# Routed experts of a hybrid layer: another order of the experts, rows of 32 turned on VectorE, modulation ahead of the gather, results scaled in two steps

## The reference

```python
def hier_moe(h, ...):                       # h = modulate(x1, sh2, sc2): normalize(x1) * (1 + sc2) + sh2
    p_g, grp = lax.top_k(softmax(t @ w_rg + b_rg), 1)          # 4 groups of experts
    p_e, local = lax.top_k(softmax(logits_in), 2)              # two of the group's 8 experts
    gate = p_g * p_e / sum(p_e)
    ...
def block_ffn(xb, e):                       # rows of one expert, width 1024 -> 512 -> 1024
    return (silu(xb @ w_gate[e]) * (xb @ w_up[e])) @ w_down[e]
# y[token] = sum over its two experts of gate * block_ffn(row);  out = LayerNorm(ALPHA * x1 + g2 * y)
```

## Time and profile before

| | us |
|---|---|
| median of 3 runs | 1691.51 (1689.35 to 1691.93) |
| the profiled execution's own time | 1683.64 |
| its span, first to last instruction | 1681.9 |

### The profile page before, as it was taken

The page is one execution under the profiler, slowest core; times in us unless marked ns, Lnnn a source line. Parts: engine busy times, 40 slices in busy tenths (PEclk is TensorE's granted clock), DMA queues, the critical chain, the costliest instruction groups (busy, mean ns, idle before and its releaser), DMA issues. The chain is left out here.

```text
span 1681.9 us, 46845 instructions
## 1 busy us (share of the span) xinstructions
PE 1495.7 (89%) x19436; PEld 1102.2 (66%) x19436; DVE 927.6 (55%) x1855; ACT 694.2 (41%) x1585; POOL 209.9 (12%) x274
## 2 busy tenths in 40 slices
PE   5799998999977899986999989964999999998768
PEld 3578886779967788874666668852656565665433
DVE  6798762332115556558989957865151553444416
ACT  5444431012235455534767745532141433533311
POOL 0000001000034445324000000000000000000024
PEclk8899999999987999997999989985999999999989
DMA  9312324542133345213011024417849789999976
GB/s 369 114 63 95 100 79 161 201 157 76 50 108 116 109 116 142 85 54 122 20 44 51 7 92 176 163 67 287 350 166 379 268 333 418 414 420 418 370 259 242
DMA packets 115265, 305.31 MB, mean 182 GB/s; under 512 B 11010, under 2 KB 57682, under 8 KB 106074
## 3 DMA queue, kind: packets, MB, share of 16 engines
q1 hardware_dynamic: 93178, 244.95, 38.7%
q0 software_dynamic: 10336, 46.67, 7.8%
q10 hardware_dynamic: 11520, 10.49, 2.0%
HBM read 256.41 MB, written 45.67 MB: 180 GB/s over the span
## 5 line engine op out<-in xcount | busy, mean ns | idle before, releaser
L2753 PE MATMUL psum<-now_hidden,i_xm 128*32 128x256 f32 x4992 | 291.9, 387 | 13.0 <-DVE now_hidden L2863 12.2
L2753 PEld LDWEIGHTS psum<-now_hidden,i_xm 128*32 128x32 f32 x4992 | 162.1, 112 | 125.5 <-DVE now_hidden L2863 16.1
L2765 PE MATMUL psum<-now_down,i_hT 128*32 128x256 f32 x2464 | 147.1, 379 | 3.1 <-ACT now_down L2820 3.0
L2879 DVE TENSOR_TENSOR i_h<-i_silu,psum 128x128 f32<-128x128 f32 x78 | 22.2, 285 | 203.0 <-ACT i_silu L2813 203.0
L2863 DVE COPY now_hidden<-raw_hidden 128x1024 f32 x168 | 104.2, 691 | 27.1 <-DMA raw_hidden<-in_w_up 18.9
L2765 PEld LDWEIGHTS psum<-now_down,i_hT 128*32 128x32 f32 x2464 | 79.7, 110 | 57.2 <-ACT now_down L2820 5.0
L2803 ACT ACTIVATE i_xm<-psum,run_mod 128x128 f32<-128x128 f32 x163 | 63.2, 455 | 121.8 <-issue 81.8
L124 PE MATMUL psum<-hT_head,wm_head 128*128 128x512 f32 (+1 forms) x256 | 96.9, 378 | 11.2 <-DVE hT_rest L415 6.9
L1918 PE MATMUL psum<-dkT,f_qT 64*128 64x512 f32 (+1 forms) x384 | 89.7, 575 | 17.4 <-ACT f_E L1968 14.9
L1968 ACT ACTIVATE f_E<-psum,f_mx 128x1280 f32<-128x1280 f32 (+2 forms) x96 | 92.9, 972 | 18.6 <-DVE f_mx L2029 17.7
L124 PE MATMUL psum<-hT_head,wm_rest 128*128 128x512 f32 (+1 forms) x256 | 95.4, 373 | 0.0
(11 more groups left out here) (378 smaller groups left out, 3027.6 us busy)
## 6 DMA issues: line engine op xcount, KB each, us to landing
raw_hidden<-in_w_gate SPq DMA_DIRECT2D x22, 2048.0 KB, 24.9
raw_hidden<-in_w_up SPq DMA_DIRECT2D x22, 2048.0 KB, 30.4
raw_down<-in_w_down SPq DMA_DIRECT2D x22, 2048.0 KB, 21.1
wa_late<-in_w_ada POOLq DMA_DIRECT2D x16, 1024.0 KB, 5.6
yb<-i_y ACTq DMA_DIRECT2D x80, 128.0 KB, 10.0
wa<-in_w_ada SPq DMA_DIRECT2D x8, 1024.0 KB, 13.6
wt<-in_w_in SPq DMA_DIRECT2D x4, 2048.0 KB, 9.1
wm<-in_w_in SPq DMA_DIRECT2D x12, 512.0 KB, 4.0
```

Of the source, the lines that this page charges most:

```text
L2753: last = nc.tensor.matmul(by_blocks(hidden_bank(s)[j * SUB:(j + 1) * SUB, :]), xm[u][:, k, s * SUB:(s + 1) * SUB], columns_of(now["hidden" ...
L2765: last = nc.tensor.matmul(down_bank(s)[j * SUB:(j + 1) * SUB, :], hT[s % 2][:, k * SUB:(k + 1) * SUB], now["down"][:, k, j * WIDE:(j + 1) ...
```

## The change

1. **Order of the experts.** The place of rank `nth` among `used` experts is now found by dealing: row `nth // 6`, column `nth % 6`, read column by column (`STRIDE = 6`). For these inputs the blocks per place were 13, 1, 1, 11, 1, 1, 9, 1, 1, 7, 1, 5, 1, 5, 1, 4, 1, 4, 1, 3, 2, 4 and become 13, 4, 1, 1, 11, 4, 1, 1, 9, 4, 1, 1, 7, 3, 1, 1, 5, 2, 1, 5, 1, 1.
2. **Modulation.** GpSimd multiplies and adds the modulation in `mixed_output`, two operations of 128x1024 per tile, and SP stores their result to `xn2`. ScalarE's `shape` is gone.
3. **Rows.** A gather takes one block: 128 partitions, each with a quarter (256 numbers) of one of 32 tokens. VectorE turns it with one transpose of 128x256 in squares of 32x32 (`turn_x`), four blocks ahead; TensorE's transposes are gone. There are four buffers (`RING`) instead of two. `tok` is computed per block: 64 products with 32 rows of weights and 96 columns instead of 16 with 128 and 24.
4. **Results.** ScalarE copies a block's result from PSUM, GpSimd multiplies it by `rep_g` in place, and ScalarE waits for that before the next silu where it waited for VectorE before (in each fourth block, from block 64 on in each).
5. **Zeros.** `mixed_output` writes zeros to all eight quads of `yb` that may stay unused; nothing is written after the experts.

```diff
+LOW = 2 * SEQ // P
 COUNT = 96
+QUARTER = 70
+AHEAD = 4
+RING = SUBS
...
-                sp.wait_ge(x_normed, t + 1)
-                sp.dma_start(xn2[t], xn[t % 2][:, :]).then_inc(xn_stored[t % 2], 16)
+                sp.wait_ge(x_shaped, t + 1)
+                sp.dma_start(xn2[t], xs[t % 2][:, :]).then_inc(xn_stored[t % 2], 16)
...
+            for w in range(2):
+                sp.dma_start(late_mod[:, w, :], d["mod_rows"][3 + w:4 + w, :].to_broadcast([P, D])).then_inc(mod_loaded, 16)
...
+                if t == 1:
+                    sp.wait_ge(nothing_ready, 1)
+                if 1 <= t <= (QUADS - LOW) // 2:
+                    for q in range(LOW + 2 * (t - 1), LOW + 2 * t):
+                        sp.dma_start(ybq[q], nothing[:, :]).then_inc(nothing_stored, 16)
...
+        def _(pool):
+            nc.gpsimd.memset(nothing[:, :], 0.0).then_inc(nothing_ready, 1)
+            pool.wait_ge(mod_loaded, 32)
+            nc.gpsimd.tensor_scalar(late_mod[:, 1, :], late_mod[:, 1, :], 1.0, None, ALU.add).then_inc(mod_ready, 1)
+            pool.wait_ge(mod_ready, 1)
+            for t in range(TL):
+                u = t % 2
+                pool.wait_ge(x_normed, t + 1)
+                if t >= 2:
+                    pool.wait_ge(xn_stored[u], 16 * (t // 2))
+                nc.gpsimd.tensor_tensor(xs[u][:, :], xn[u][:, :], late_mod[:, 1, :], ALU.mult).then_inc(x_scaled, 1)
+                pool.wait_ge(x_scaled, t + 1)
+                nc.gpsimd.tensor_tensor(xs[u][:, :], xs[u][:, :], late_mod[:, 0, :], ALU.add).then_inc(x_shaped, 1)
...
-        link(ts(some_long[:, :], nblk[:, :], LONG - 0.5, None, ALU.is_gt))
-        link(red(threes[:, :], some_long[:, :], AX, ALU.add))
-        link(ts(by_three[:, :], used[:, :], 1.5, -0.5, ALU.mult, ALU.add))
-        link(stt(by_two[:, :], used[:, :], 2.0, threes[:, :], ALU.mult, ALU.subtract))
-        link(ts(by_two[:, :], by_two[:, :], -1.0, None, ALU.add))
+        nearest(whole[:, :], used[:, :], 1.0 / STRIDE, 0.5 / STRIDE - 0.5)
+        link(stt(left[:, :], whole[:, :], -float(STRIDE), used[:, :], ALU.mult, ALU.add))
+        tt(used_number[:, :], number, some[:, :], ALU.mult)
...
-        ts(short[:, :], nth, -1.5, by_three[:, :], ALU.mult, ALU.add)
-        ts(key[:, :], nth, -2.0, by_two[:, :], ALU.mult, ALU.add)
-        link(ts(pos[:, :], nth, 2.0, threes[:, :], ALU.mult, ALU.add))
-        link(tt(short[:, :], short[:, :], key[:, :], ALU.max))
-        link(stt(pos[:, :], nth, 3.0, pos[:, :], ALU.mult, ALU.min))
-        link(tt(pos[:, :], pos[:, :], short[:, :], ALU.min))
-        link(ts(pos[:, :], pos[:, :], -0.25, None, ALU.add))
-        link(ts(pos[:, :], pos[:, :], EXACT, None, ALU.add))
-        link(ts(pos[:, :], pos[:, :], -EXACT, None, ALU.add))
+        nearest(row_of[:, :], nth, 1.0 / STRIDE, 0.5 / STRIDE - 0.5)
+        link(stt(column_of[:, :], row_of[:, :], -float(STRIDE), nth, ALU.mult, ALU.add))
+        link(stt(pos[:, :], column_of[:, :], left[:, :], row_of[:, :], ALU.min, ALU.add))
+        link(stt(pos[:, :], column_of[:, :], whole[:, :], pos[:, :], ALU.mult, ALU.add))
...
+            tt(row_hot[:, here, :], is_row[:, here, :], ids[:, :].unsqueeze(2).to_broadcast([P, TL, SUB]), ALU.mult)
+            tt(part_hot[:, here, :], part_of[:, here].unsqueeze(2).to_broadcast([P, TL, BLOCKS]),
+               small[:, COUNT:COUNT + BLOCKS].unsqueeze(1).to_broadcast([P, TL, BLOCKS]), ALU.is_equal).then_inc(picked, 1)
...
-        cp(tok[:, 0:QUADS], m.bank(2, QUADS)).then_inc(token_ready, 1)
+        ts(tok[:, 0:BLOCKS], m.bank(2, BLOCKS), float(SUBS), small[:, QUARTER:QUARTER + 1], ALU.mult, ALU.add).then_inc(token_ready, 1)
...
-            last = nc.tensor.matmul(m.bank(2, QUADS), row_hot[:, n, :], part_hot[:, n, :], start=(n == 0), stop=(n == PICKS - 1))
+            for a in range(SUBS):
+                last = nc.tensor.matmul(m.bank(2, BLOCKS)[a * SUB:(a + 1) * SUB, :], row_hot[:, n, :], part_hot[:, n, :], start=(n == 0), stop=(n == PICKS - 1),
+                                        tile_position=(0, a * SUB))
...
-        def gather(q, i, u):
-            pool.wait_ge(x_turned[u], i)
-            pool.indirect_dma_start(out=xg[u][:, :], out_offset=None, in_=d["xn2"],
-                                    in_offset=bass.IndirectOffsetOnAxis(ap=tok[:, q:q + 1], axis=0)).then_inc(gathered[u], 16)
+        def gather(b):
+            pool.wait_ge(x_turned, b - RING + 1)
+            pool.indirect_dma_start(out=xg[b % RING][:, :], out_offset=None, in_=quarters(d["xn2"]),
+                                    in_offset=bass.IndirectOffsetOnAxis(ap=tok[:, b:b + 1], axis=0)).then_inc(gathered[b % RING], 16)
+
+        def scale(b, u, s):
+
+            pool.wait_ge(y_kept, b + 1)
+            nc.gpsimd.tensor_tensor(yo[u][:, s, :], yo[u][:, s, :], rep_g[:, :], ALU.mult).then_inc(y_scaled, 1)
+
+        def body(q, i, u, s):
+            b = q * SUBS + s
+            gather(b + AHEAD + RING)
+            scale(b, u, s)
 
         pool.wait_ge(routed, 1)
-        nc.gpsimd.memset(nothing[:, :], 0.0).then_inc(nothing_ready, 1)
-        blocks(pool, start=lambda q, i, u: gather(q + 2, i + 1, u))
+        pool.wait_ge(gate_loaded, 16 * SUBS)
+        for b in range(AHEAD):
+            gather(b + RING)
+        nb = blocks(pool, block=body)
+        for u in range(RING):
+            pool.wait_ge(gathered[u], ((nb + AHEAD + 2 * RING - 1 - u) >> 2) * 16)
...
+        def keep_y(b, i, u, s):
+            act.wait_ge(used["down"], b * KE + KE)
+            if s == 0:
+                act.wait_ge(stored[u], 16 * SUBS * i)
+            nc.scalar.activation(yo[u][:, s, :], down_bank(s), ACT.Copy).then_inc(y_kept, 1)
...
-        def keep_y(b, i, u, s):
-            dve.wait_ge(used["down"], b * KE + KE)
-            if s == 0:
-                dve.wait_ge(stored[u], 16 * SUBS * i)
-            nc.vector.tensor_tensor(yo[u][:, s, :], down_bank(s), rep_g[:, :], ALU.mult).then_inc(y_kept, 1)
...
+        def turn_x(b):
+
+            dve.wait_ge(gathered[b % RING], 16 * (b // RING) + 16)
+            if b >= RING:
+                dve.wait_ge(used["hidden"], (b - RING + 1) * KD)
+            nc.vector.transpose(xm[b % RING][:, :, :], run_columns(xg[b % RING])).then_inc(x_turned, 1)
...
-            keep_y(b, i, u, s)
+            turn_x(b + AHEAD)
```

133 lines of the change are left out of this document (50 added, 83 removed).

## The result

The changed kernel takes 1712.46 us (median of 4 runs, 1711.14 to 1719.63) against 1690.43 us of the kernel before in the same session: ratio 1.0152, 95% interval 1.0124 to 1.018. A second session, with the same kernel unedited, gave 1.0098 (1.0075 to 1.0121; medians 1707.85 against 1689.02). These ratios are not the quotients of the two medians, which would be 1.0130 and 1.0111. So the changed kernel is slower by 1.0 to 1.5%; the medians lie 22.0 and 18.8 us apart. 1679 was forecast. The two intervals do not overlap, so a ratio from one session and one from another can differ by half a per cent with no edit at all.

A forecast was written before the change was run, and what follows sets the result against it. TensorE (19.6 us per expert) and the weight queue (17.4) were taken as close bounds in the experts. Terms -14.8 + 1.0 + 1.7 + 0.3 - 0.6 + 0 = -12.4 us took 1691.51 to 1679.1; 8-in-10 range 1668 to 1692.

The forecast's parts named there:

- 3.7 us: Inside an expert block, the chain from silu through transposes and gather issue to GpSimd's multiplication; 1.5 us spare, costed at nothing.
- The exclusion: GpSimd's block operations and VectorE's weight copies getting in each other's way in SBUF: +1.0 us, bounds 0 to 35.
- `mixed_output`, +2.0: In `mixed_output`, +1.7 us for 1 MB loaded earlier at the start, +0.3 for a later store at the end.
- The experts, -14.8: From the experts to `combine`: earlier end without TensorE's transposes and with the new order, less the longer result path, -14.8 us.
- the 28.4 available: Between expert blocks, twenty sets of TensorE transposes at 1.42 us, all that removing them can give: 28.4 us.
- the replay: Block-by-block model of the experts' weight queue; put TensorE's end near 1601.5 us, 16 earlier, 3 of them from the order.
- Combine would begin at 1613.3.: Behind the experts, `combine` beginning 9.75 us after the first last store, at 1613.3 instead of 1628.12 us.
- the near 0 and -0.6: Routing: fewer small VectorE operations, -0.6 us; `tok` products and start of the first block, 0 (-3 to +6).
- The rival named last: In expert blocks, GpSimd's operations lengthened or held by VectorE's make ScalarE's silu late: +19.5 us, 1698.6; chance 0.12.

The follow-up runs named there:

- scaling on VectorE: Changed kernel with one VectorE operation taking the result from PSUM and multiplying it, replacing ScalarE's copy and GpSimd's multiplication; ratio 1.001 to the kernel before.
- one column: Changed kernel with GpSimd's multiplication of the result cut from 256 columns to one; ratio 1.0087 to the kernel before.
- the multiplication that nobody waits for: Changed kernel with the result scaled by VectorE, plus an unused GpSimd multiplication of 128x256 per block; ratio 1.0029 to the kernel before.

## Why the prediction was wrong

**"3.7 us, where ScalarE's next silu is due 5.18 us behind the last ... I cost it at nothing."** This step failed first. 5.18 us is the time of a block inside an expert, and there it held (median 5.18). But the chain was added up without the copies. At a change of expert they stand in VectorE's queue ahead of both transposes; GpSimd's gather waits for the second of them, the multiplication stands behind the gather, ScalarE behind the multiplication. The cover that I named is missing just where it is needed: at the first change the silu was 3 us late, and scaling on VectorE gave 18 to 26 us of blocks back, the hold included, where I had this path at 0 and the hold at 1.0. With the hold gone (one column), 13 us of it remained; the runs let 6 of them go with the hand-over and 7 with ScalarE's copy, which I had counted only once, at the end, but this division is within the spread.

**The exclusion, +1.0 of 0 to 35.** My choice near the lower end was wrong: a copy that overlaps the multiplication takes 1.41 us instead of 0.68. By the rule that the prediction takes from the Trainium skill, "SBUF — State Buffer", section "SBUF: two separate sides" (an exclusive lock of the two engines' ports), that is what had to be expected, and the trace agrees: in 18 of 21 meetings the copy ended behind the multiplication, in three the multiplication was stretched. In VectorE's time it was 14.4 us; on the path 8 to 13 by the one-column run, which shortens the chain too, and 5.5 by the multiplication that nobody waits for, which one profile cannot tell from nothing. "No row shows the two in each other's way" was no argument for nothing, since no row had them at work together.

**`mixed_output`, +2.0.** Measured +10.0 and +12.0. I asked what GpSimd's 5 us per tile hold back in its own chain and found slack, which is so; I did not ask what they do to VectorE beside them, 0.6 us in each steady tile. The early loads were costed at 1.7 us; about 5 are left when GpSimd's operations go, and they vanish when the loads go too. Loading them later in the changed kernel gave only 1.4 to 3.4 back. The fall of the granted clock I did not foresee either; what it cost at the end of this stretch was not isolated.

**The experts, -14.8.** The relief is real but smaller: with scaling on VectorE against the kernel before, both in the dealt order, blocks fall from 440.6 to 430.2 us, 10.4 of the 28.4 available. The rest is in part at the changes, where VectorE and not TensorE is the bound: copies 4.9, product and transpose 0.6, result 0.4 and rows 0.65 are 6.5, measured 6.3, where the three without the rows were 5.9 before; and in part where the weights are. For the dealt order in the kernel before, the replay was right on the blocks to some 3 us (1.2 later forecast, 2.0 shorter measured), but not on the end: the last copy came 13.4 us later, at 1609.4, and the end was 7.9 us longer, 8 us in the time where I had 0.

**"Combine would begin at 1613.3."** It began at 1658. I let the last stores take 9.75 us as before, with 5.2 MB of loads done by 1610. The loads started at 1628.2 instead, behind the late last copy, and ran beside the last stores, issued from 1645.0 and not from 1603.5; and behind the last gather stands a drain of 7.0 us. In the kernel before GpSimd's drain (10.2 us, from 1584.5) was over 33 us ahead of `combine`. I had counted GpSimd's instructions and not what its leaving costs.

**What was right.** The product for `tok` took 4.67 us (4 to 9 forecast as what would show the prediction, 7 taken in the sum), `tok` to block 0 shrank by 2 to 3 us and the routing grew by 1, near the 0 and -0.6. The zeros in `mixed_output` cost nothing. The rival named last had the right engine and the right sign; at 1698.6 it lacked the mixed output and the end. A silu waiting for `i_y` (17.2 us, 6 times) and copies above 0.69 us, which were to prove it, are both in the trace.

## What to carry to other kernels

Add up a chain through in-order queues in the worst block, with what stands ahead of each link there, not in the steady one. Work given to an idle GpSimd is not free while VectorE moves SBUF data: look for each VectorE operation that would run at the same time, in every phase, and count those of the held kinds (here weight copies and products of two SBUF tensors), one per GpSimd operation. And look at how an engine leaves a phase: its last, even useless, transfer sets when its drain starts.

## What the runs showed of the hardware

- A VectorE copy of 128x1024 within SBUF, or a product of two SBUF tensors, that meets a GpSimd multiplication or addition mostly ends 0.55 us behind it: 0.69 us became 1.41 on average (21 copies), 0.69 became 1.36 (five products of 128x512). Others that overlapped GpSimd's work in the same profile did not change: L1812 with an operand in PSUM (746 ns), the transposes of 128x256 within SBUF (six, 0.61 us) and `BATCH_NORM_STATS2` on one SBUF tensor (seven, 0.695).
- It goes the other way too, though less: GpSimd's gather issue took 1.14 us beside a copy and 0.98 otherwise, its multiplication of one column 0.51 and 0.20, and three of its multiplications of 128x256 took 0.9 to 1.2 us instead of 0.74.
- GpSimd's drain at the end of the experts took 7.00 us in the thirteen profiles with gathers per block up to the end and 6.68 in the three without the last four; it began 3.4 to 8.2 us behind the last gather's issue. In the kernel before, which does not wait for the gather's landing first, it took 10.2 us from the issue on. VectorE's took 0.05 to 0.08 us, ScalarE's 0.01.
- GpSimd's multiplication of 256 columns took 750 ns, of one column 0.20 us away from VectorE's copies (272 ns over all 77). ScalarE's operation of 128x32 within SBUF took 400 ns, eight in a row 2.54 us.
- 128 passes of 32 rows by 96 columns took 4.67 us, 36 ns each, nearly all of them at a granted clock of 1.2 GHz.
